# A transformer block and two hybrid layers in one kernel: where ScalarE's function tables are loaded

## The reference, cut to what matters

```python
for l in range(2):
    h = rms_norm(x, norm_w[l])
    x = x + hybrid_mixer(h, ...)

# hybrid_mixer
qkv = silu(depthwise_conv_centred(qkv, qkv_conv_w))
q = l2_normalize(q); k = l2_normalize(k)
g = -exp(a_log) * softplus(a_lg + dt_bias); beta = sigmoid(b_lg)
o = gated_delta_chunked(q, k, v, g_fwd, beta_fwd) + the same run backwards
o = o * rsqrt(mean(o * o) + EPS) * dn_norm_w
y_a = (o * silu(z_a)) @ w_dn_out
u = depthwise_conv_centred(cf_val * sigmoid(cf_glu), cf_conv_w) + cf_conv_b
y_b = (silu(layer_norm(u)) * silu(z_b)) @ w_cf_out
gate = sigmoid(gate_lg + gate_b)
y = (gate[..., 0, :] * y_a + gate[..., 1, :] * y_b) @ w_out
```

## Time and profile before

| what | us |
|---|---|
| runs | 2153.76, 2154.81, 2158.68 (median 2154.81) |
| span of the profiled execution, its own time in the profile | 2153.7 |
| TensorE busy | 2067.3 (96%) |
| VectorE, ScalarE, GpSimd busy | 1253.4, 858.8, 907.2 |

### The profile page before, as it was taken

One profiled execution on the slowest core, in us unless ns is written; L12 is line 12 of the kernel. 1 busy time (PEld: TensorE's weight loads), 2 busy tenths in 40 slices (PEclk: granted clock), 3 DMA queues, 4 the chain that ended last, 5 costly groups with the idle time before them and its releaser, 6 DMA issues.

```text
span 2153.7 us, 26713 instructions
## 1 busy us (share of the span) xinstructions
PE 2067.3 (96%) x10772; PEld 1644.9 (76%) x10772; DVE 1253.4 (58%) x1944; ACT 858.8 (40%) x1373; POOL 907.2 (42%) x431
## 2 busy tenths in 40 slices
PE   8999999999999999999999899999999999999997
PEld 7888888776656688888888677787778787778775
DVE  5422223756686643222223988989853679898753
ACT  4222233323444543222233475444443475344632
POOL 4444444332123344444444564434434563444442
PEclk9999999999999999999999999999999999999998
DMA  4333333321101232333333222111223222100222
GB/s 156 111 135 94 95 97 98 108 69 39 37 24 50 66 94 94 98 98 98 98 97 95 73 78 79 59 30 31 59 88 98 79 88 78 50 22 29 79 88 78
DMA packets 46186, 169.09 MB, mean 79 GB/s; under 512 B 5232, under 2 KB 6000, under 8 KB 45808
## 3 DMA queue, kind: packets, MB, share of 16 engines
q1 hardware_dynamic: 45344, 165.60, 24.4%
q10 hardware_dynamic: 720, 1.79, 0.2%
HBM read 165.27 MB, written 2.10 MB: 78 GB/s over the span
## 4 chain that ended last, share of the span: by engine, by line
PE 74%; DVE 18%; ACT 5%; issue 1%; POOL 0%; DMA 0%; DVEq 0%; ACTq 0%
PE ps L385 21%; PE ps L387 20%; PE ps L386 20%; DVE cu L1834 4%; DVE blk_t L1936 2%; DVE outer L1934 1%; PE ps L632 1%; PE ps L648 1%; PE ps L617 1%; PE ps L441 1%; ACT whi L1002 1%; DVE rn L1503 1%; ACT dl L1433 1%; PE ps L952 1%; DVE dl L2043 1%
## 5 line engine op out<-in xcount | busy, mean ns | idle before, releaser
L2163 POOL TENSOR_TENSOR wlo<-raw,whi 128x1024 fp32r<-128x1024 f32 x300 | 751.9, 2513 | 871.2 <-ACT whi L1002 870.8
L385 PE MATMUL ps<-xh,whi 128*128 128x512 f32 x1584 | 640.9, 405 | 14.8 <-ACT gates L1177 6.2
L387 PE MATMUL ps<-xh,wlo 128*128 128x512 f32 x1584 | 619.5, 391 | 0.0
L386 PE MATMUL ps<-xl,whi 128*128 128x512 f32 x1584 | 619.5, 391 | 0.0
L385 PEld LDWEIGHTS ps<-xh,whi 128*128 128x128 f32 x1584 | 298.6, 189 | 108.1 <-issue 36.5
L1002 ACT CAST whi<-raw 128x1024 fp32r<-128x1024 f32 x300 | 312.3, 1043 | 155.2 <-DMA raw<-in_stream 155.1
L387 PEld LDWEIGHTS ps<-xh,wlo 128*128 128x128 f32 x1584 | 298.5, 188 | 63.9
L386 PEld LDWEIGHTS ps<-xl,whi 128*128 128x128 f32 x1584 | 299.2, 189 | 59.6 <-issue 3.1
L1834 DVE SCALAR_TENSOR_TENSOR cu<-up,lcols,cu 128x512 f32<-128x512 f32 x180 | 173.2, 1013 | 0.1
L2199 POOL TENSOR_TENSOR cu<-cu,prod 128x512 f32<-128x512 f32 x60 | 87.6, 1460 | 138.0 <-ACT prod L1244 136.7
L1540 DVE TENSOR_TENSOR ml<-mid,mh 128x512 fp32r<-128x512 f32 x42 | 56.4, 1348 | 152.6 <-ACT mh L1063 152.6
(11 more groups left out here) (356 smaller groups left out, 3008.3 us busy)
## 6 DMA issues: line engine op xcount, KB each, us to landing
raw<-in_stream SPq DMA_DIRECT2D x300, 512.0 KB, 3.6
w1k<-in_w SPq DMA_DIRECT2D x1, 2048.0 KB, 8.4
w1v<-in_w SPq DMA_DIRECT2D x1, 2048.0 KB, 8.0
outT<-h SPq DMA_DIRECT2D x4, 512.0 KB, 2.7
h<-in_xT ACTq DMA_DIRECT2D x2, 512.0 KB, 7.8
h<-in_xT SPq DMA_DIRECT2D x2, 512.0 KB, 7.6
mats<-in_mats ACTq DMA_DIRECT2D x1, 448.0 KB, 10.7
msk<-in_masks SPq DMA_DIRECT2D x1, 258.0 KB, 3.9
```

Source lines behind the costliest of these rows:

```text
L385: pe.matmul(out, wh, hi, start=first, stop=False)
L386: pe.matmul(out, wh, lo, start=False, stop=False)
L387: return pe.matmul(out, wl, hi, start=False, stop=last)
L2163: pool.tensor_tensor(m.wlo[:, slot, :], m.raw[:, slot, :], m.whi[:, slot, :].bitcast(F32), ALU.subtract).then_inc(s.wlo)
```

## The change

A helper `load_tables(set_name)` puts a table load at a place of the program's choice, and it is called in front of waits. For logarithm and exponential it names one set that has both. Where the active set already has the function of the next activation, the build adds no load of its own, but a load that the source asks for is always made.

```diff
--- before.py
+++ after.py
@@ -34,6 +34,7 @@
 
 UNIT = 8 * P
 RING = 4
+LN_EXP, SIGMOID, SILU, SQRT = "natural_log_exp_and_others", "sigmoid_and_others", "silu_and_others", "sqrt_and_others"
 AHEAD = 2
 
 ROPE_AT = {u: r for r, u in enumerate((2, 3, 4, 5, 6, 7, 11, 12, 13, 14, 15))}
@@ -993,6 +994,10 @@
 
         act.wait_ge(s.act_step, step(ins))
 
+    def load_tables(set_name):
+
+        act.preload_act_table_set(set_name)
+
     def weights_upto(u):
 
         nonlocal split
@@ -1024,6 +1029,7 @@
         act.activation(square_row(m, e, k), m.h[:, k, :], ACT.Square).then_inc(s.square)
 
     def root(e):
+        load_tables(SQRT)
         act.wait_ge(s.sums, e + 1)
         act.activation(m.rn1[:] if e == 3 else m.rn[:], ps[:, 6, :], ACT.Sqrt, bias=eps, scale=1.0 / D).then_inc(s.root)
 
@@ -1042,6 +1048,7 @@
         e = 2 * f
         weights_upto(u0 + AHEAD + 2)
         root(e)
+        load_tables(SILU)
         for i in range(NF):
             weights_upto(u0 + 2 * i + AHEAD + 1)
             act.wait_ge(s.g_scaled, NF * f + i + 1)
@@ -1212,6 +1219,8 @@
             for k in range(KD):
                 act.copy(m.xh[:, k, :], m.qall[:, k, :]).then_inc(s.mix_hi)
         y = m.m1_y if mixer else m.m2_y
+        if mixer:
+            load_tables(SIGMOID)
         for c in range(KD):
             p = c % 2
             weights_upto(u0 + c + AHEAD + 1)
@@ -1284,6 +1294,7 @@
 
         def inverse_lengths(count, bank, scale):
 
+            load_tables(LN_EXP)
             act.wait_ge(s.len_sum, count)
             then(act.activation(ps[:, bank, :], ps[:, bank, :], ACT.Ln, bias=eps, scale=scale))
             act.activation(m.roots[:], ps[:, bank, :], ACT.Exp, scale=-0.5).then_inc(s.len_root)
@@ -1346,6 +1357,8 @@
         def z_unit(n):
             u = u0 + L_Z + n
             weights_upto(u + AHEAD + 1)
+            if n in (0, 2, 6):
+                load_tables(SILU)
             act.wait_ge(s.unit, u + 1)
             z = m.z_o if n < 4 else m.z_cu
             act.activation(z[:, n % 4, :], ps[:, Z_BANKS[n % 3], :], ACT.Silu).then_inc(s.filled)
@@ -1408,6 +1423,8 @@
             for n, t0, t1 in DELTA_SLOTS[i, point]:
                 if t0 == 0:
                     weights_upto(U0_LAYER[l] + L_GATE + n + AHEAD + 1)
+                    if n % 2 == 0:
+                        load_tables(SIGMOID)
                 if t1 == KD:
                     gate_unit(l, n)
             if point in SHARED_POINTS and pooled < CF_TAPS:
```

## The result

| what | us |
|---|---|
| runs of the kernel before, same chip | median 2157.55 (2153.76 to 2161.70, 7 runs) |
| runs of the changed kernel | median 2167.03 (2164.30 to 2170.11, 7 runs) |
| ratio | 1.0044, 95% interval 1.0033 to 1.0055 |
| span of the profiled executions, before and after | 2153.7 and 2168.8 |

The change costs 9.5 us by these medians (7.1 to 11.9 by the interval). It is slower, as forecast, but by more than the 6.0 of the sum, and the changed kernel's median lies 1.0 above the end of the range and 6.2 above the forecast of 2160.8. Of these 6.2, 3.5 are the size of the change; the other 2.7 are the starting point, since the three runs of before that the forecast stood on had a median of 2154.81, and seven have 2157.55.

A forecast was written before the change was run, and what follows sets the result against it. The chain was read as 74% TensorE, 18% VectorE, 5% ScalarE. Terms +3.5 (chunks 1 to 3) and +2.5 (entry), others 0, made +6.0 on 2153.7, 2159.7; with 1.1 up to the median, 2160.8, range 2152.0 to 2166.0.

The forecast's parts named there:

- Chunks 1 to 3: With the load gone from their second half they become like chunk 0: 0.58 later each, +3.5 us for both layers.
- the sigmoid 1.6 behind the copies: Sign of being right: in all eight chunks the gate's sigmoid starts 1.6 behind the level-2 copies.
- the taps at 4.1: Sign of being right: VectorE's two taps behind L2102 take about 4.1 in every chunk.
- eight waits of 1.0: Sign of being right: TensorE's waits on L2110 go from 2 to 8, of 1.0 each.
- the update 16.9 behind: Sign of being right: VectorE's L2118 follows the copies by 16.9 in every chunk.
- Entry of chunk 0: The decays' load runs while ScalarE waits, GpSimd arrives 0.84 earlier: 1.23 later per layer, +2.5 us.
- one hold more: At chunk 0's entry VectorE's second L2067 waits for a `wlo`: 2.07, less GpSimd's lead of 0.84, is 1.23 per layer.
- passed on whole, since L908 waits for it: +2.5 us: At chunk 0's entry VectorE's 1.23 delay per layer reaches TensorE in full, through its wait for the inverses.
- three loads between logarithm and exponential: Lead units, `z` units and layer norm: 1.28 each off ScalarE, each covered, 0; without the last cover -1.3 a layer.
- loads that change sides: Loads that only change sides of a logarithm or of one split: 0.
- starved split: Rival, 30 taps behind chunk 3: one or two `wlo` per layer get in, 2.07 each, 2164.9 to 2169.1; chance 0.18.
- rival on the faster side: VectorE's tap stays in front of GpSimd's in chunks 1 to 3: 2152.6, or 2150.9 with the entry's better bound; chance 0.16.

The follow-up runs named there:

- gate's load back: Changed kernel with the gate's sigmoid load behind the level-2 copies again and chunk 0 without its extra load: 2161.39 us, ratio 1.0011 to the kernel before.
- Exp loads back: Changed kernel with the exponential set loaded again between logarithm and exponential: 2169.45 us, ratio 1.0043 to the kernel before.
- decays' load back: Changed kernel with the load of chunk 0's decays behind its waits again: 2162.31 us, ratio 1.0012 to the kernel before.
- entry filled: Changed kernel with unused matmuls before TensorE's two waits at chunk 0's entry: six and three 2169.05 us, ratio 1.0050; three and one 2163.64 us, ratio 1.0032.
- both back: Changed kernel with the gate's sigmoid load and chunk 0's decays' load both back in their old places: 2155.81 us, ratio 0.9997 to the kernel before.
- second profile: The kernel before, run and profiled once more without edit: 2158.10 us, ratio 1.0003; the profiled execution took 2153.33 us.
- split later still: Changed kernel with decays' load back, GpSimd's tap product behind the scaled keys, weight split and second product behind the new values' copies: 2153.39 us, ratio 0.9981.

## Why the prediction was right in its mechanism and short in its sum

**Chunks 1 to 3: right.** Each sign that the prediction named came: the sigmoid 1.6 behind the copies, the taps at 4.1, eight waits of 1.0, the update 16.9 behind. The term was +0.58 a chunk; the period from update to update grew by 0.59 to 0.63, in all +3.7 for both layers against 3.5. The experiment that takes the load back turns it to zero.

**Entry of chunk 0: the hold right, the step from it to TensorE's time failed.** I took +1.23 a layer for one hold more. With the clock kept up the entry cost +1.16 and +1.21. That this agrees so well is luck: GpSimd's lead over VectorE grew by 1.23 rather than the 0.84 that I had, and with it my own sum gives 2.07 - 1.23 = 0.84, where VectorE's two instructions took 1.08 more and the elimination ahead of them 0.17. What failed is the step "passed on whole, since L908 waits for it: +2.5 us": the sum took a wait of TensorE to cost its length and no more. The term measured +5.9 (2.79 and 3.08). The waits grew from 1.9 and 1.0 to 3.1 and 1.65, and in eight of eight layers with about these waits the clock fell at or behind them (the changed kernel twice, gate's load back, Exp loads back), against two of fourteen in the kernels whose entry has the old waits. Shorter waits (decays' load back) and work put into the long ones (entry filled) both took the fall away, so at this place the longer waits bring it. In the changed kernel that is 1.6 and 1.9 on top, +3.5 for both layers.

**The end of the layer: a term that the sum left out without a reason.** It is +1.19 and +1.37, by a fall of the clock behind waits that the change leaves alone. The kernels closest to before (its two executions, both back) show it in one layer of six, all others in eighteen of twenty. The experiments exclude the Exp loads; undoing either the gate's load or the decays' load alone does not remove it, and the one profile with both undone is without it. The first wait there is 1.9 in all thirteen profiles. What decides whether the clock falls stays open.

**The three loads between logarithm and exponential, and the loads that change sides: right at 0, as far as the runs can tell.** Both back leaves only them, at 0.9997 (0.9988 to 1.0006).

**The rivals.** The starved split did not get in: three `wlo` took 16.50 in the changed kernel, against 15.24, and the stretch with the 30 taps is unchanged to 0.02. My reading of the earlier trace rows was off, though: it is not the first two that find no way in until the taps are done, but the first alone. It took 11.82 (10.54 before), and the two behind it, after the taps, 2.4 each. This rival's band held the measured time, for a wrong reason. The rival on the faster side needed GpSimd to lose its lead of 0.50 over VectorE's taps in chunks 1 to 3; it was 0.53. The starved splits, GpSimd in the changed kernel, all three and then the first alone:
```profile
1545.33 16.50 POOL L2180 TENSOR_TENSOR wlo<-raw,whi 128x1024 fp32r<-128x1024 f32 x3 [5.54 <-ACT whi L1007]
1545.33 11.82 POOL L2180 TENSOR_TENSOR wlo<-raw,whi 128x1024 fp32r<-128x1024 f32 x1 [5.54 <-ACT whi L1007]
```

**The account.** 3.7 in the chunks, 2.4 at the entry by VectorE, 3.5 at the entry by the clock, 2.6 at the end by the clock: 12.1 against the first profile of before. Why the runs give 9.5 and not 12.1 or more is open. The kernel before loses time at the same two places in some executions, 2.4 us in its second profile, but elsewhere it gains and loses more: the two profiles of the changed kernel agree in the table to 0.1 and differ in span by 4.8 (2168.8 and 2164.0). The kernel before took 2153.8 to 2161.7 in its seven runs, and in the 75 runs of it beside the experiments the mean granted clock goes with the time (0.991 to 0.993 up to 2156.0, 0.986 to 0.990 above). That spread is more than any term of my sum. It also moved the starting point by 2.7 between three runs and seven, and the range should have been drawn from it too.

## What to carry to other kernels

Before moving work earlier on an engine that feeds another, ask which resource the receiver will take when it gets going: here ScalarE's gain of 0.79 let GpSimd in front of VectorE and cost 0.59 a chunk. Put such blocks where the blocked engine has idle time anyway; that move, and not the table loads, made the kernel 6.3 us faster. A wait of TensorE that grows can cost more than it grows by: look at the granted clock behind it, in more than one execution of the kernel before. And compare two profiles stretch by stretch, since their spans also hold what the clock did elsewhere.

## What the hardware showed that I had not expected

The granted clock falls behind waits that differ little: not in the first profile of before at 1.9 and 1.0, but in one layer of the second at the same waits, and always at 3.1 and 1.65. The length of a wait alone does not decide it: behind the wait of 3.55 in the first feed-forward part the clock stayed full in both profiles of before. At the entry and the end of a layer a fall lasts some 3 to 7 us and costs 0.4 to 2.4, the latter in layer 1 of the kernel with the split later still. Matmuls with no use, placed in the wait, prevent it at the entry (four layers of four, in two of them they outlasted the wait).

The Trainium skill, "SBUF — State Buffer", section "SBUF: two separate sides", has the one that starts first hold the shared port pair for its whole instruction, while the other fully blocks. Four taps at 6.56 among three instructions of GpSimd of 7.08 in sum agree with blocks of that kind. But one `wlo` that took 11.82 amid VectorE's back-to-back taps, where the two behind it took 2.4, shows again that to have asked is not to be served next.

A table load takes 1283 ns with the next activation some 10 ns behind it (at the decays of chunk 0 of the changed kernel, load 1357.30, sigmoid 1358.59), whether it stands in front of a wait or behind it.
